# A hybrid attention/mLSTM layer on one core: the mLSTM output projection by a seven-product scheme

## The chip, the cores and the metric

The kernel runs on one core of a Trainium2 chip, as one launch. The metric is the device time of that launch in microseconds. Three runs of the kernel before took 1912.51 us in the median (1910.1 to 1913.47).

## The reference

One inference step of one layer, for a prompt of 512 tokens and 8 sample sequences of 8 tokens (T = 576 token columns together), model width 2048. Two mixers run side by side on one projection of the input, and are merged:

```
h = rmsnorm(x, norm_pre) * (1 + scale(c)) + shift(c)
u = h @ w_in                                   # columns: both mixers' inputs and the gates g_a, g_m
y_a = (att * silu(z_a)) @ w_br_a               # 1024 -> 2048, attention half of the branch
y_m = (sigmoid(o_m) * hm * silu(z_m)) @ w_br_m # 1024 -> 2048, mLSTM half of the branch
y = (sigmoid(g_a) * y_a + sigmoid(g_m) * y_m) @ w_out
out = x + gate(c) * rmsnorm(y, norm_post)
```

All is float32. Keys, values and the mLSTM state are outputs too, but the change does not touch them.

## The kernel before

A float32 product is computed as three products of rounded parts: each operand is split into a high part (`hi`, rounded by the scalar engine) and the rest (`lo`, subtracted by the vector engine), and TensorE adds hi*hi, hi*lo and lo*hi into PSUM. Work is written out by hand per engine, and the engines meet on counting semaphores. One step of the weight stream is called a granule, numbered x; `S_F` is the first granule of the branch, `S_G` the first of the last product `@ w_out`, `S_END` the end.

**The gate stage** (128 granules, just ahead of the branch) computes the two gates' columns with a seven-product scheme (Strassen's, in Winograd's form): a 2x2 block product in 7 instead of 8 block products. Its granule is 21 matmuls, 128x128 by 288 columns. SyncE loads raw weights for two granules at a time (two transfers of 256 KB, `form_load`, L584) into one of three buffers `w_all`. The vector engine builds four more weight forms by sums (`forms_a` L2201, `forms_b` L2206 and L2207), the scalar engine rounds (`f_hi`), the vector engine subtracts (`f_lo`, L2212). After 8 granules the seven PSUM results are combined on the vector engine (`products_a`, `products_b`, L2225 to L2244).

**The branch** (64 granules) is a plain product. The 2048 output features are taken in four quads of 512. Each quad has a half-matrix of 8 granules for attention (`ya`) and then one of 8 for mLSTM (`ym`), so that ya and ym alternate. A granule (`wide_granule`) is one row block of the weights, 128x512: 4 blocks of 3 matmuls with 512 prompt columns, and 2 for the 64 sample columns with the roles of the operands exchanged (`s_part`). At a half-matrix's end `mix` multiplies the four PSUM blocks by the gates (L2310) and adds ya and ym (L2315). The sample part is transposed back by 4 small matmuls (`fold_features`, L1190) one granule after the half-matrix's end. Raw weights come through a ring of four 256 KB slots, `w_raw`.

**The last product** (64 granules, also 14 matmuls each) takes its stationary operand from `y_all`, which is split from `g_a` in groups of four.

The order on the vector engine is that of one loop over x: in iteration x it makes the low part of granule x+3, then whatever else falls in that iteration. Each engine takes its instructions strictly in that order. The scalar engine's loop is the same with the high part, which waits until TensorE has used the slot.

Of the kernel before, what the change touches and what calls it, by code (L numbers as in the profile page):

```python
# [101 lines left out]
def mat_of(x):  # L102

    for m, (i, kind, first, n) in enumerate(MATS):
        if first <= x < first + n:
            return m, i, kind, x - first, n
# [24 lines left out]
def build(nc, x_prompt, x_sample, cache_k, cache_v, state_C, state_n, state_m, page_table, c_prompt, c_sample,  # L131
# [13 lines left out]
    with ctx:  # L145
# [36 lines left out]
        brm = [sb(f"brm{k}", "R3" if k < 4 else "R2", (4 + k if k < 4 else k - 4) * 2 * T, [P, 2 * T], F32R) for k in range(8)]  # L182
# [190 lines left out]
        g_a = wk("g_a", [P, 4, T], off=0)  # L373
        g_m = wk("g_m", [P, 4, T])
        s_copy = wk("s_copy", [P, QW], off=8 * T + QW)
# [14 lines left out]
        def back(q):  # L390
            if q < 4:
                return att_back[:, q % 2, :]
            return (y_back if q % 4 < 2 else rows_back)[:, q % 2, :]

        def wide_pair(x):
            if x >= S_END - 2:
                return end_hi[x - S_END + 2], end_lo[x - S_END + 2]
            return w_hi[:, slot_of(x)], w_lo[:, slot_of(x)]
# [70 lines left out]
        in_att, IN_ATT = (in_k, in_v), 32 * NB  # L469
        in_ga, IN_GA = in_n0, 16  # L470
# [14 lines left out]
        def _(sp):  # L485
# [80 lines left out]
            def load_rows(src, kt, col, slot):  # L566
                sp.dma_start(w_raw[:, slot].rearrange("p t c -> p (t c)"), src[kt * P:(kt + 1) * P, bass.ds(col, QW)])\
                  .then_inc(raw_ready[slot], 16)

# [20 lines left out]
            def branch_quad(i, n1):  # L590
                col_br = n1 * QW - QW
                for j in range(FGRAN):
                    sp.wait_ge(lo_ready, S_F + FGRAN * i + j - RING + 1)
                    if j < KT // 2:
                        load_rows(wba, j, col_br, slot_of(j))
                    else:
                        load_rows(wbm, j - KT // 2, col_br, slot_of(j))

            sp.wait_ge(lo_ready, S_F - 2)
            with sp.Fori(1, FQ + 1) as i:  # L600
                branch_quad(i - 1, i)

            def out_quad(q):
                col = sp.snap(q * QW)
                for kt in range(KT):
                    sp.wait_ge(lo_ready, S_G + q * KT + kt - RING + 1)
                    load_rows(wo, kt, col, slot_of(kt))

            with sp.Fori(0, FQ) as q:
                out_quad(q)  # L610
# [10 lines left out]
        def _(pe):  # L621
# [544 lines left out]
            def wide_granule(m, x, of, first, last):  # L1166

                hi, lo, both = of
                for b in range(4):
                    if first:  # L1170
                        if m:
                            pe.wait_ge(bank_free[b // 2], V0 + 32 + 2 * m - 1 + b % 2)
                        else:
                            pe.wait_ge(p_free, 7 * (GP - 1) + (4, 6, 7, 7)[b])
# [5 lines left out]
                if first and m:  # L1180
                    pe.wait_ge(s_copied, m)
# [11 lines left out]
            def branch_quad(i):  # L1193
                for j in range(FGRAN):
                    m, _, kind, kt, n = mat_of(S_F + FGRAN * i + j)
                    pe.wait_ge(lo_ready, S_F + FGRAN * i + j + 1)
                    if not i:
                        pe.wait_ge(br_lo, j + 1)
                    of = parts((bra if kind == "ya" else brm)[kt])
                    wide_granule(m, S_F + FGRAN * i + j, of, kt == 0, kt == n - 1)  # L1200
                    if kt == 1 and m:
                        fold_features(m - 1)

            for i in range(FQ):
                branch_quad(i)
# [11 lines left out]
            def out_quad(q, kts):  # L1217
                m = NM + q
                for kt in range(kts):
# [6 lines left out]
                    for tt in range(NT):  # L1226
                        if first:
                            pe.wait_ge(bank_free[tt // 2], V0 + 32 + 2 * m - 1 + tt % 2)
                        rows = slice(tt * P, (tt + 1) * P)
# [4 lines left out]
                    if first:  # L1234
                        pe.wait_ge(s_copied, m)
                    s_part(x, both, first, last)
                    if kt == 1 and not q:
                        fold_features(m - 1)
# [23 lines left out]
        def _(act):  # L1262
# [297 lines left out]
            def br_hi_of(q):  # L1560
# [8 lines left out]
                go((bra[q] if q < 8 else brm[q - 8])[:, 0:T], back(q)).then_inc(br_hi, 1)  # L1569

            def split_first(x):

                act.wait_ge(gemm_used, S_F - 2 if x < S_F + 2 else S_F)
                split_hi(slot_of(x), (x - GG) // RING, x)

            for g in range(GG):
# [14 lines left out]
                if g >= GG - 2:  # L1591
                    split_first(S_F + g - GG + 2)
# [819 lines left out]
        def _(pool):  # L2412
# [258 lines left out]
            for q in (2, 3, 4, 6):  # L2671
                back_load(q)
# [54 lines left out]
```

## Time and profile before

| | |
|---|---|
| median of 3 runs | 1912.51 us |
| profiled execution: its time / its span | 1909.96 us / 1908.5 us |
| TensorE busy | 1878.3 us (98%) |
| VectorE busy | 993.6 us (52%) |
| ScalarE busy | 684.5 us (36%) |
| gate stage | 1126 to 1484 us |
| branch | 1484 to 1692 us |
| last product | 1692 to 1901 us |

A busy engine is one that executes. Where a row of the timeline starts before the row above it has ended, the two overlap in the engine's pipeline: the distance from start to start is then what an instruction costs in a dense row, and its duration is when its result is there. Matmul ends are modelled.

### The profile page before, as it was taken

Reading aid. Unit: us, or ns where it says so; the run is one execution under the profiler, and the core shown is the slowest. Engines: PE = TensorE matmul, PEld = TensorE weight load, DVE = VectorE, ACT = ScalarE, POOL = GpSimd, SP = SyncE. Lnnn points to the kernel's source line nnn. Section 1 sums busy time; section 2 is a strip of 40 time slices with the busy share of each in tenths; the row PEclk is TensorE's granted clock in tenths of the full one; section 3 lists DMA queues with packets and bytes.
Section 4 is the critical chain, followed back from the end, with each engine's and each line's share of the span. In section 5 each row is a group of like instructions: output and inputs, shape, how many; then the busy total and the mean of one; then the engine's idle time right before and its main releaser. Section 6 shows DMA issues by size and latency. Waiting matters only on the chain.

```text
span 1908.5 us, 32997 instructions
## 1 busy us (share of the span) xinstructions
PE 1878.3 (98%) x13093; PEld 1684.8 (88%) x13093; DVE 993.6 (52%) x2026; ACT 684.5 (36%) x1136; POOL 201.9 (11%) x343
## 2 busy tenths in 40 slices
PE   6999999999999999999999999999999999999998
PEld 4779898988899999888899999999999888888886
DVE  4666234336563334554445767777777544443234
ACT  4312222234445453543333333344334422223332
POOL 2111001200002100111331000000000100000000
PEclk9999999999999999999999999999999999999999
DMA  9996573323224543233443334343444634443223
GB/s 318 319 288 200 186 228 112 78 67 101 55 83 141 172 155 100 74 84 120 118 138 94 104 119 124 113 125 118 133 121 125 230 128 133 132 166 95 83 78 132
DMA packets 188157, 261.88 MB, mean 137 GB/s; under 512 B 15706, under 2 KB 146906, under 8 KB 186858
## 3 DMA queue, kind: packets, MB, share of 16 engines
q1 hardware_dynamic: 167344, 194.03, 33.8%
q0 software_dynamic: 18432, 65.74, 10.4%
q8 instruction: 97, 1.59, 0.3%
q10 hardware_dynamic: 2242, 0.19, 0.1%
q14 instruction: 42, 0.34, 0.1%
HBM read 231.55 MB, written 28.35 MB: 136 GB/s over the span
## 4 chain that ended last, share of the span: by engine, by line
PE 93%; SPq 2%; DMA 2%; DVE 1%; POOL 1%; ACT 1%; issue 0%; DVEq 0%; ACTq 0%; POOLq 0%
PE gemm L623 67%; PE bank_s L623 12%; PE bank_a L623 6%; PE bank_o L623 5%; SPq L499 2%; DMA ada_in<-in_w_ada 1%; PE bank_s L876 1%; PE bank_s L652 1%; PE bank_a L820 0%; DVE y_tok L2397 0%; DMA w_raw<-in_w_in 0%; PE bank_s L1041 0%; POOL hm_sq L2595 0%; POOL hm_sq L2594 0%; PE bank_o L674 0%
## 5 line engine op out<-in xcount | busy, mean ns | idle before, releaser
L1264 ACT ACTIVATE w_hi<-w_raw 128x512 fp32r<-128x512 f32 x382 | 239.9, 629 | 689.3 <-PE gemm L623 406.7
L1676 DVE TENSOR_TENSOR w_lo<-w_raw,w_hi 128x512 fp32r<-128x512 f32 x382 | 268.4, 703 | 415.6 <-ACT w_hi L1264 415.0
L623 PE MATMUL gemm<-h_hi,w_hi 128*128 128x288 f32 x2048 | 461.1, 307 | 1.2 <-DVE dec_tok L1957 0.5
L623 PE MATMUL gemm<-h_hi,w_lo 128*128 128x288 f32 x2048 | 438.7, 296 | 0.0
L623 PE MATMUL gemm<-h_lo,w_hi 128*128 128x288 f32 x2048 | 437.3, 295 | 0.0
L623 PEld LDWEIGHTS gemm<-h_hi,w_hi 128*128 128x128 f32 x2048 | 328.2, 189 | 49.3 <-issue 42.8
L623 PEld LDWEIGHTS gemm<-h_hi,w_lo 128*128 128x128 f32 x2048 | 329.1, 188 | 0.0
L623 PEld LDWEIGHTS gemm<-h_lo,w_hi 128*128 128x128 f32 x2048 | 328.8, 188 | 0.0
L1264 ACT ACTIVATE f_hi<-w_all 128x896 fp32r<-128x896 f32 x128 | 120.0, 950 | 180.4 <-PE gemm L623 104.3
L2212 DVE TENSOR_TENSOR f_lo<-w_all,f_hi 128x896 fp32r<-128x896 f32 x128 | 139.4, 1089 | 63.5 <-ACT f_hi L1264 63.1
L623 PE MATMUL gemm<-w_hi,y_all 128*128 128x512 f32 x496 | 153.6, 391 | 0.0
L623 PEld LDWEIGHTS gemm<-w_hi,y_all 128*128 128x128 f32 x496 | 92.8, 188 | 22.9
L623 PE MATMUL gemm<-w_lo,y_all 128*128 128x512 f32 x248 | 96.7, 390 | 0.0
L623 PE MATMUL gemm<-bra,w_hi 128*128 128x512 f32 x256 | 79.4, 391 | 0.0
L623 PE MATMUL gemm<-brm,w_hi 128*128 128x512 f32 x256 | 79.4, 391 | 0.0
L623 PE MATMUL gemm<-s_hi,f_lo 128*128 128x288 f32 x256 | 75.6, 295 | 0.0
L623 PE MATMUL gemm<-s_hi,f_hi 128*128 128x288 f32 x256 | 75.4, 295 | 0.0
L623 PE MATMUL gemm<-s_lo,f_hi 128*128 128x288 f32 x240 | 70.8, 295 | 0.0
L1970 DVE CUSTOM_DVE_ANT_0 e_map<-bank_s,alibi 128x128 f32<-128x128 f32 (+3 forms) x64 | 31.4, 491 | 53.5 <-PE bank_s L623 52.3
L623 PEld LDWEIGHTS gemm<-bra,w_hi 128*128 128x128 f32 x256 | 47.7, 188 | 12.1 <-issue 0.2
L623 PEld LDWEIGHTS gemm<-brm,w_hi 128*128 128x128 f32 x256 | 47.7, 188 | 11.8 <-issue 0.2
L2643 POOL DMA_DIRECT2D gate_scratch<-h_free x32 | 22.1, 746 | 315.5 <-ACT h_free L1264 315.5
(538 smaller groups left out, 3112.5 us busy)
## 6 DMA issues: line engine op xcount, KB each, us to landing
w_raw<-in_w_in SPq DMA_DIRECT2D x256, 256.0 KB, 2.9
ada_in<-in_w_ada SPq DMA_DIRECT2D x72, 512.0 KB, 8.0
w_all<-in_w_in SPq DMA_DIRECT2D x128, 256.0 KB, 3.2
w_raw<-in_w_out SPq DMA_DIRECT2D x64, 256.0 KB, 2.5
gate_scratch<-h_free POOLq DMA_DIRECT2D x32, 288.0 KB, 3.1
ada_gate<-in_w_ada SPq DMA_DIRECT2D x16, 512.0 KB, 5.3
k_page<-in_cache_k POOLq DMA_DIRECT2D x16, 512.0 KB, 5.3
v_page<-in_cache_v POOLq DMA_DIRECT2D x16, 512.0 KB, 4.6
```

Of the source, the lines that this page charges most:

```text
L499: sp.dma_start(ada_slot(n)[:, :, half * CW:(half + 1) * CW], w_ada2[r * AQ * P:(r + 1) * AQ * P, col:col + CW] .rearrange("(t p) c -> p t ...
L623: return nc.tensor.matmul(out, lhsT, rhs, start=start, stop=stop, skip_group_check=True)
L652: nc.tensor.transpose(banks[0][:, j * P:(j + 1) * P], src[:, j * P:(j + 1) * P], ident[:])
L876: done = nc.tensor.transpose(bank_s[:, j // 2, (j % 2 * PAGES + pg) * P:(j % 2 * PAGES + pg + 1) * P], k_page[:, pg, h * P:(h + 1) * P], i ...
L1264: return nc.scalar.activation(out, in_, func, **kw)
L1676: V.tensor_tensor(w_lo[:, slot], w_raw[:, slot], w_hi[:, slot], ALU.subtract).then_inc(lo_ready, 1)
L1970: link(V.tensor_tensor_reduce(e_map[:, s % 2, c, 0:n], bank_s[:, c, 0:n], alibi[:, TP - n:TP], 1.0, LOW, ALU.add, ALU.max, mx[:, s % 2, c: ...
L2212: V.tensor_tensor(f_lo[wslot_of(g)][:], w_all[g // 2 % WRING][:, g % 2, P:8 * P], f_hi[wslot_of(g)][:], ALU.subtract).then_inc(lo_ready, 1)
L2643: pool.dma_start(gate_scratch[i // 8, 2 * (i % 8) + cb].rearrange("p (a t) -> p a t", a=2), h_free[:].rearrange("p (k e) t -> p k e t", e= ...
```

## The change

The mLSTM half of the branch is computed by the seven-product scheme, and the order of the half-matrices becomes ya0 to ya3, then ym0 to ym3. A ym granule (`pair_granule`) is 21 matmuls with 288 columns that cover prompt and samples alike; four such granules (the 1024 inputs are 8 row blocks, taken two by two) complete a pair of column blocks, 128 features each, and the seven results are combined (`m_products_a`, `m_products_b`) and gated (`gate_pair`, at the granules of a table, `GATED_AT`). The activations' sums and splits are made once, in the first two ya half-matrices (`brm_sums`, `brm_hi_of`, `brm_lo_of`). Raw ym weights for two granules at a time come into one of two buffers, `w_form`, of which the second lies over the whole of `w_raw`. `y_all` is split one block per granule, two granules ahead of its use, and the gates of ya lie in four buffers `y_f` that also hold the sum.

```diff
-MATS = [(i, kind, S_F + FGRAN * i + first, KT // 2) for i in range(FQ) for kind, first in (("ya", 0), ("ym", KT // 2))]
+BRANCH = (("ya", 0), ("ya", 1), ("ya", 2), ("ya", 3), ("ym", 0), ("ym", 1), ("ym", 2), ("ym", 3))
+MATS = [(i, kind, S_F + FGRAN * k, FGRAN) for k, (kind, i) in enumerate(BRANCH)]
+KX = KT // 4
+GATED_AT = ((0, MATS[4][2] + 5), (1, MATS[5][2] + 1), (2, MATS[5][2] + 5), (3, MATS[6][2] + 1), (4, MATS[6][2] + 5),
+            (5, MATS[7][2] + 1), (6, S_G + 1), (7, S_G + 3))
...
+        w_form = [sb("w_form0", "h_hi", 0, [P, 2, 8 * P]), sb("w_form1", "w_raw", 0, [P, 2, 8 * P])]
...
 # SyncE
+            def pair_load(k, b):
+                i, _, first, _ = MATS[k]
+                x = first + 2 * b
+                if b % 2:
+                    sp.wait_ge(lo_ready, RAW_FREE[x])
+                elif k == 4 and not b:
...
+                else:
+                    sp.wait_ge(lo_ready, x - 2 if b else form_before(k) + 6)
+                col = i * QW + b // 2 * CW
+                for s in range(2):
+                    row = (4 * (b % 2) + 2 * s) * P
+                    sp.dma_start(w_form[b % 2][:, s, 0:4 * P].rearrange("p (t c) -> p t c", t=2),
+                                 wbm[row:row + 2 * P, col:col + CW].rearrange("(t p) c -> p t c", p=P)).then_inc(in_form[b % 2], 16)
...
 # TensorE
+            def pair_granule(m, a, n, j, x):
+                pe.wait_ge(lo_ready, x + 1)
+                if not n:
+                    pe.wait_ge(br_lo, KT // 2 + j + 1)
+                wh, wl = f_hi[SLOT[x]], f_lo[SLOT[x]]
+                for k, (of, part) in enumerate(((0, 0), (5, 4), (2, 1), (4, 5), (6, 2), (3, 3), (1, 6))):
+                    if j == 0:
+                        bank_wait(m, a, n, k)
+                    cols = slice(of * P, (of + 1) * P)
+                    hi, lo = brm_hi[j][:, part, :], brm_lo[j][:, part, :]
+                    for i, (w, h) in enumerate(((wh, hi), (wh, lo), (wl, hi))):
+                        done = mm(m_banks[k], w[:, cols], h, start=j == 0 and i == 0, stop=j == KX - 1 and i == 2)
+                    if j == KX - 1 and k < 6:
+                        done.then_inc(p_done, 1)
+                done.then_inc(gemm_used, 1)
...
 # ScalarE
+            def pair_hi(x):
+                b = mat_of(x)[3] // 2
+                act.wait_ge(m_made, ...)
+                act.wait_ge(gemm_used, SLOT_FREE[x])
...
+                go(f_hi[SLOT[x]][:], w_form[b % 2][:, x % 2, P:8 * P]).then_inc(hi_ready, 1)
...
 # VectorE
+            def gate_pair(n):
...
+                link(V.scalar_tensor_tensor(c, g, 1.0, c, ALU.add, ALU.mult))
+                V.tensor_tensor(y, y, c, ALU.add).then_inc(mix_ready, 1)
...
             for x in range(S_F, S_END):
                 m, i, kind, kt, n = mat_of(x)
-                if x + LOOKAHEAD < S_END - 2:
-                    split_lo(slot_of(x + LOOKAHEAD), x + LOOKAHEAD)
...
+                ends = kind == "ym" and kt % KX == KX - 1
+                y = x + LOOKAHEAD
+                sums = is_form(y) and mat_of(y)[3] % 2 == 0
...
+                if sums:
+                    pair_a(b)
+                    if not ends:
+                        pair_b(b)
+                if ends:
+                    m_products_a(2 * i + kt // KX)
+                if is_form(x + 2):
+                    pair_lo(x + 2)
+                if ends:
+                    m_products_b(2 * i + kt // KX, x)
+                    if sums:
+                        pair_b(b)
...
+                if y < S_END - 2 and not is_form(y) and not (late and kt == n - 2):
+                    row_lo(y)
...
+                if x - S_F - 6 in range(0, 2 * KX, 2):
+                    brm_sums((x - S_F - 6) // 2)
+                if x - S_F - 7 in range(0, 2 * KX, 2):
+                    brm_lo_of((x - S_F - 7) // 2)
...
+                for n_pair, at in GATED_AT:
+                    if x == at:
+                        gate_pair(n_pair)
...
+                if kind == "ya" and kt == n - 1:
+                    mix(a)
```

Two places on the vector engine show how it lands in the program. First, the middle of the branch. Before, from the end of a ya half-matrix (`g_a`) to that of the ym half-matrix after it (`g_m`):

```order
L2310 SCALAR_TENSOR_TENSOR g_a<-g_a,gemm 128x512 x4
L1676 TENSOR_TENSOR w_lo<-w_raw,w_hi 128x512 x3
L2320 TENSOR_REDUCE s_copy<-bank_s 128x256
L2328 SCALAR_TENSOR_TENSOR g_a<-g_a,s_copy 128x4x64
L1676 TENSOR_TENSOR w_lo<-w_raw,w_hi 128x512 x5
L2310 SCALAR_TENSOR_TENSOR g_m<-g_m,gemm 128x512 x4
L2315 TENSOR_TENSOR g_a<-g_a,g_m 128x512 x4
```

Eight granules need eight `w_lo`, and the gating stands once per half-matrix.

Now, in the ym half-matrices, four granules make one cycle. This is its first half, the iteration that forms the weights of the next two granules but one, with a gating in it (`w_form_77` and `w_form_78` are the two buffers, `c_buf` the combined results):

```order
L2491 TENSOR_TENSOR w_form_77<-w_form_77 128x2x256
L2496 TENSOR_TENSOR w_form_77<-w_form_77 128x2x128
L2497 TENSOR_TENSOR w_form_77<-w_form_77 128x2x128
L2503 TENSOR_TENSOR f_lo_110<-w_form_78,f_hi_107 128x896
L2550 SCALAR_TENSOR_TENSOR c_buf_258<-g_m,c_buf_258 128x1152
L2551 TENSOR_TENSOR y_f_73<-y_f_73,c_buf_258 128x1152
L2503 TENSOR_TENSOR f_lo_109<-w_form_77,f_hi_106 128x896
```

The fourth row is the last reader of buffer 78, so that its next load starts behind it; the second half of the cycle begins with the forms in that buffer:

```order
L2491 TENSOR_TENSOR w_form_78<-w_form_78 128x2x256
L2517 TENSOR_TENSOR m_u_80<-m_p_79,bank_o 128x288
L2521 TENSOR_TENSOR c_buf_259<-m_p_79,gemm 128x288
L2524 TENSOR_TENSOR m_u_81<-m_u_80,gemm 128x288
L2503 TENSOR_TENSOR f_lo_111<-w_form_77,f_hi_108 128x896
L2531 TENSOR_TENSOR c_buf_259<-m_u_81,gemm 128x288
L2533 TENSOR_TENSOR c_buf_259<-m_u_81,gemm 128x288
L2534 TENSOR_TENSOR m_u_80<-m_u_80,gemm 128x288
L2537 TENSOR_TENSOR c_buf_259<-m_u_80,bank_s 128x288
L2496 TENSOR_TENSOR w_form_78<-w_form_78 128x2x128
L2497 TENSOR_TENSOR w_form_78<-w_form_78 128x2x128
L2503 TENSOR_TENSOR f_lo_110<-w_form_78,f_hi_107 128x896
```

The last two rows of sums stand directly ahead of the low part that is made from them.

Second, the end of the first ya half-matrix, iteration S_F+7. Before (`brm` are mLSTM activations, split as they come):

```order
L1676 TENSOR_TENSOR w_lo<-w_raw,w_hi 128x512
L2172 TENSOR_TENSOR brm_67<-rows_back,brm_67 128x512
L2173 TENSOR_TENSOR brm_67<-rows_back,brm_67 128x64
L2310 SCALAR_TENSOR_TENSOR g_a<-g_a,gemm 128x512 x4
L1676 TENSOR_TENSOR w_lo<-w_raw,w_hi 128x512
```

And now:

```order
L2442 TENSOR_TENSOR w_lo<-w_raw,w_hi 128x512
L2482 TENSOR_TENSOR brm_lo_69<-y_back,brm_hi_65 128x288
L2483 TENSOR_TENSOR brm_lo_69<-y_back,brm_hi_65 128x576
L2485 TENSOR_TENSOR brm_lo_69<-m_new,brm_hi_65 128x1152
L2565 SCALAR_TENSOR_TENSOR y_f_73<-y_f_73,gemm 128x512 x4
L2442 TENSOR_TENSOR w_lo<-w_raw,w_hi 128x512
```

Larger splits of activations stand ahead of the four operations that free the PSUM blocks.

## Rows read from the trace of the kernel before

**Rows 1.** The page, busy time and share of each engine:

```profile
PE 1878.3 (98%) x13093; PEld 1684.8 (88%) x13093; DVE 993.6 (52%) x2026; ACT 684.5 (36%) x1136; POOL 201.9 (11%) x343
```

**Rows 2.** Windows: length, busy (count) by engine, PE clock, DMA share, GB/s:

```profile
1236.00:1484.00 248.00, 248.00 (x1872) 247.96 (x1870) 188.45 (x306) 100.59 (x116) 17.71 (x26) 1.00 0.41 122
1484.00:1692.00 208.00, 207.96 (x927) 167.69 (x926) 98.27 (x179) 59.21 (x97) 10.26 (x14) 1.00 0.44 148
```

**Rows 3.** The chain that ended last: start us, us, what:

```profile
1137.66 1.20 PE gemm L623 x9
...
1296.40 1.20 PE gemm L623 x9
...
1506.86 2.73 PE gemm L623 x12
...
1510.06 2.72 PE gemm L623 x12
...
1516.42 0.44 PE bank_s L1190 x4
1516.86 2.75 PE gemm L623 x12
...
1542.86 2.75 PE gemm L623 x12
```

**Rows 4.** Timeline, VectorE, gate stage: start, us, operation [idle before <- releaser]:

```profile
1415.51 0.45 DVE L2225 TENSOR_TENSOR h_free<-h_free,bank_s 128x288 f32<-128x288 f32 x1 [0.95 <-ACT h_free L1264]
...
1416.61 1.08 DVE L2212 TENSOR_TENSOR f_lo<-w_all,f_hi 128x896 fp32r<-128x896 f32 x1
1417.61 0.45 DVE L2238 TENSOR_TENSOR h_free<-h_free,gemm 128x288 f32<-128x288 f32 x1
...
1418.89 0.46 DVE L2244 TENSOR_TENSOR h_free<-h_free,gemm 128x288 f32<-128x288 f32 x1
1419.26 0.42 DVE L2206 TENSOR_TENSOR w_all<-w_all 128x256 f32<-128x256 f32 x1
...
1421.16 1.09 DVE L2212 TENSOR_TENSOR f_lo<-w_all,f_hi 128x896 fp32r<-128x896 f32 x1 [1.02 <-ACT f_hi L1264]
1422.17 0.68 DVE L2201 TENSOR_TENSOR w_all<-w_all 128x512 f32<-128x512 f32 x1
1422.89 0.43 DVE L2206 TENSOR_TENSOR w_all<-w_all 128x256 f32<-128x256 f32 x1
...
1423.69 1.08 DVE L2212 TENSOR_TENSOR f_lo<-w_all,f_hi 128x896 fp32r<-128x896 f32 x1
```

**Rows 5.** Timeline, ScalarE, the same stretch:

```profile
1420.17 0.95 ACT L1264 ACTIVATE f_hi<-w_all 128x896 fp32r<-128x896 f32 x1 [3.92 <-DVE w_all L2207]
...
1421.87 1.15 ACT L1264 ACTIVATE h_free<-h_free 128x1152 f32<-128x1152 f32 x1
```

**Rows 6.** Groups of instructions by form, VectorE: count | busy us, mean ns | idle:

```profile
L2192 DVE TENSOR_TENSOR s_lo<-s_new,s_hi 128x1152 fp32r<-128x1152 f32 x7 | 9.5, 1352 | 0.0
```

**Rows 7.** Loads of `w_all`: one pair's issues; landing of all, 1239.9's, 1269.3's:

```profile
L584 SPq DMA_DIRECT2D w_all<-in_w_in x2: 368/424/479, 1424.8 to 1425.2; - x2
DMA to landing us min/median/max: 2.7/3.2/5.4
DMA to landing us min/median/max: 3.2/3.2/3.2
DMA to landing us min/median/max: 3.7/3.7/3.7
```

**Rows 8.** Timeline at S_F+7, ScalarE and VectorE:

```profile
1506.96 0.63 ACT L1264 ACTIVATE w_hi<-w_raw 128x512 fp32r<-128x512 f32 x1 [1.99 <-PE bank_s L623]
1507.50 0.67 ACT L1264 ACTIVATE brm<-rows_back 128x576 fp32r<-128x576 f32 x1
...
1508.97 2.47 DVE L2310 SCALAR_TENSOR_TENSOR g_a<-g_a,gemm 128x512 f32<-128x512 f32 x4
```

**Rows 9.** Windows, the start of the program; columns as in rows 2:

```profile
10.00:20.00 10.00, 5.72 (x30) 5.72 (x31) 4.78 (x10) 7.46 (x9) 1.21 (x3) 1.00 1.09 301
```

More of the change, by code:

```diff
@@ L588, in _ @@
                 form_load(b)
[L590 to L601, printed above, removed]
@@ new lines, in form_before @@
+            def form_before(k):
+                return max(first for _, kind, first, _ in MATS[:k] if kind == "ym")
+            for k, (i, kind, first, n) in enumerate(MATS[:len(BRANCH)]):
+                then = MATS[k + 1][1]
+                if kind == "ya":
+                    for j in range(n):
+                        if j or not follows_form(first):
+                            row_load(wba, first + j, j, i * QW)
+                        if j == 3 and then == "ym":
+                            pair_load(k + 1, 0)
+                    if then == "ym":
+                        pair_load(k + 1, 1)
+                else:
+                    for b in range(0 if MATS[k - 1][1] == "ym" else 2, 4):
+                        if b == 3 and then != "ym":
+                            row_load(wba if then == "ya" else wo, first + n, 0, MATS[k + 1][0] * QW)
+                        pair_load(k, b)
@@ L605, in out_quad @@
+            for q in range(FQ):
                 for kt in range(KT):
[L606 to L610, printed above, removed]
+                    if q or kt:
+                        row_load(wo, S_G + q * KT + kt, kt, q * QW)
             for nth, tt in enumerate(LAST_ORDER):
@@ L1164, in s_part, with pairs_before, wide_granule @@
                 mm(bank_s[0:NS, 0, :], both[:, 0:NS], wl, start=False, stop=last).then_inc(gemm_used, 1)
-            def wide_granule(m, x, of, first, last):
+            def pairs_before(m):
+                return GP + sum(2 for _, kind, _, _ in MATS[:m] if kind == "ym")
+            def wide_granule(m, a, x, of, first, last):
                 hi, lo, both = of
@@ L1191, in fold_features @@
                 done.then_inc(s_folded, 1)
[L1193 to L1202, printed above, removed]
@@ new lines, in _ @@
+            a = n = 0
+            for m, (i, kind, first, count) in enumerate(MATS[:len(BRANCH)]):
+                for kt in range(count):
+                    if kind == "ya":
+                        pe.wait_ge(lo_ready, first + kt + 1)
+                        if not m:
+                            pe.wait_ge(br_lo, kt + 1)
+                        wide_granule(m, a, first + kt, parts(bra[kt]), kt == 0, kt == count - 1)
+                    else:
+                        pair_granule(m, a, n + kt // KX, kt % KX, first + kt)
+                    if kt == 1 and m and MATS[m - 1][1] == "ya":
+                        fold_features(a - 1)
+                if kind == "ya":
+                    a += 1
+                else:
+                    n += 2
@@ new lines, in _ @@
+                if ends:
+                    m_products_b(2 * i + kt // KX, x)
+                    if sums:
+                        pair_b(b)
+                b += sums
+                if y < S_END - 2 and not is_form(y) and not (late and kt == n - 2):
+                    row_lo(y)
+                elif S_END - 2 <= y < S_END:
+                    end_split_lo(y)
+                if 4 <= x - S_F + 3 < 8:
+                    br_lo_of(x - S_F + 3)
+                if x - S_F - 6 in range(0, 2 * KX, 2):
+                    brm_sums((x - S_F - 6) // 2)
```

408 lines of the change are left out of this document (283 added, 125 removed).

## The prediction

> **What bounds the kernel now.** I read the page's busy times first: TensorE is busy 98% of the span, VectorE 52% [rows 1]. Then the windows by stage: in the gate stage TensorE is busy 248.0 of 248 us with VectorE at 188 (76%), in the branch 207.96 of 208 with VectorE at 98 (47%) [rows 2]. So TensorE sets both paces, but the stage that already uses the seven-product scheme has much less room beside it. Third, the chain of waits for the price of a granule [rows 3]. In the gate stage the same piece starts at 1137.66 and, 57 granules later, at 1296.40: 2.785 us for 21 matmuls of 288 columns. In the branch two granules start 3.195 us apart, for 14 matmuls of 512 columns, a half-matrix takes 1542.86 - 1516.86 = 26.00 us, and of that 0.44 us is the four transposes of the sample part. Last, the timelines of VectorE and ScalarE in the gate stage, because the change puts that pattern where results are combined twice as often.
>
> **TensorE alone.** 32 ym granules go from 3.195 to 2.785 us: -13.1 us. The transposes stand after 8 half-matrices before and after 4 now: -1.8 us. Together -14.9 us, if TensorE never waits.
>
> **What VectorE has to do.** Costs are distances from start to start in dense stretches of rows 4. Per granule one `f_lo` of 896 columns: 1421.16 to 1422.17, 1.01 us. Per two granules the forms: `pair_a` 0.72 (1422.17 to 1422.89), `pair_b` 0.80 (1422.89 to 1423.69). Per four granules the seven combinations: three take 1415.51 to 1416.61, 1.10 us, four 1417.61 to 1419.26, 1.65 us. The gate stage pays those once in eight granules. New is `gate_pair`, two dependent operations of 1152 columns: one such takes 1.352 us [rows 6]; the first counts with 0.04 more for the wait between them, the second with 0.08 less for the overlap, 2.66 us. Six of the eight fall inside the ym stretch.
>
> Now the cycle of four granules in the order in which the change's rows stand. Half one: forms 1.52, `f_lo` 1.01, `gate_pair` 2.66, `f_lo` 1.01: 6.20 us. Half two: `pair_a` 0.72, then what the gate stage shows word for word: 1415.51 to 1422.17, 6.66 us, for the three combinations, an `f_lo`, the four combinations, `pair_b`, and an `f_lo`. That stretch holds an idle 1.02 us [rows 4]: `pair_b` comes last, the next `f_lo` needs the high part of just these forms, and ScalarE starts it only at `pair_b`'s end, 0.95 us of work [rows 5]. Half two is 7.38 us. The cycle is 13.6 us, and TensorE needs 4 x 2.785 = 11.1 us. In the gate stage this hole is hidden by eight granules' room (22.3 us); here it is not.
>
> **The load inside the cycle.** The gate stage has three weight buffers, the ym stage two. A buffer's load starts when the `f_lo` of its second granule ends; VectorE has in between only one `f_lo`, and the gating in half one, before it stands at the forms that need the data. From that end to the issue 0.03 us, the second transfer is issued 0.4 later (1424.8, 1425.2), and it lands after 3.2 us in the pair at 1239.9, 3.7 in that at 1269.3, 3.4 in the mean of nine pairs [rows 7]: 3.88 us in all, with the wake-up. Half one then takes 1.52 + 1.09 + 3.88 = 6.49 us instead of 6.20. In half two the load (0.72 + 1.10 + 1.09 + 3.88 = 6.79) fits in 7.38. Cycle: 13.9 us. Bounds: with the fastest landing of 2.7 the load is hidden and the cycle is 13.6; at 5.4 it lasts through both halves, 8.5 + 8.8 = 17.3 us. I take the mean of the nine, since the ym stretch has fewer other transfers than the gate stage with its stores.
>
> [...]
>
> **The ym stretch, summed.** Zero is TensorE's start of the first ym granule. VectorE has the first two granules ready by then; the third's high part must wait until TensorE has left the last ya granule, so the first regular forms start at 0.95 + 0.08 + 1.01 = 2.0 us. The first cycle has no gating but the samples' reduction of ya3, about 1.1 us, and waits once for ScalarE: I follow it through to 14.6 us. Five more cycles, 69.5, to 86.1. The last forms' cycle frees TensorE's last bank only by its fourth combination: 6.49 + 0.72 + 1.10 + 1.00 + 1.28 + 0.46 = 11.1, then one product 0.4 and three granules 8.4, in all 19.9. TensorE leaves ym at 106.0 us. By itself it would need 32 x 2.785 + 0.44 = 89.6, so +16.4 us. The first two granules of the last product wait 0.8 us for the last combinations and low parts.
>
> **The end of the first ya half-matrix.** In iteration S_F+7 the splits of the first mLSTM activations stand ahead of `mix` on VectorE. Before, `mix` began at 1508.97, 2.0 us after ScalarE's `w_hi` of that granule (1506.96), and 1.1 us before TensorE wanted the first block, at 1510.06 [rows 3, 8]. Now ScalarE first rounds 288, 576 and 1152 columns: it starts on them 0.54 after `w_hi` [rows 8] and needs about 0.30 + 0.57 + 1.15 (1.15 for 1152 columns [rows 5]; the others are durations of 0.41 and 0.67 less the overlap). VectorE follows with 0.37 + 0.67 + 1.27 (1.352 less 0.08), and the first block of `mix` takes 0.68. From TensorE's start of the granule: 0.10 + 0.54 + 2.02 + 0.04 + 2.31 + 0.68 = 5.7 us, where TensorE comes for the block at 3.2. It waits 2.5 us, once; the later ends of ya have no such splits. At the least it is 0, if ScalarE's roundings ran ahead (its loop does not let them), at the most about 4 with a late load of the rows.
>
> **What costs nothing.** The splits of `y_all` (0.74 on VectorE, 0.6 on ScalarE per granule) stand in granules where VectorE has 0.6 of 3.2 us to do; the two gatings in the last product add 2.7 each and use up the lead there, not more. The cover is two granules of lead; without it they would cost about 1 us each. POOL and SyncE only issue.
>
> **Sum.** -14.9 + 16.4 + 0.8 + 2.5 = +4.8 us. The profiled execution took 1909.96, so it would take 1914.8; against the median 1912.51 that is 1917.3 us. The profiled execution lies 2.6 us under the median, inside the spread of the three.
>
> **The rivals.** (1) VectorE keeps up and TensorE sets the pace: -14.9 + 2.5, 1900 us. For it: the gate stage runs this pattern with TensorE never idle. Against: 13.6 us of VectorE's queue per 11.1 us. It would need the gating to cost nearly nothing and the hole of 1.02 to close. 10%. (2) The load is hidden and `mix` is not late: -14.9 + 14.6 + 0.8, 1913 us: 22%. For it: landings of 2.7 to 3.0 occur. (3) The side of a clear loss: the loads land late. One place: the forms of half one behind the pair's landing. Three gate loads of 1152 KB run while pairs are on their way, and landings of 5.4 have been seen [rows 7]. From a landing of 3.2 on each 0.1 us costs 0.6 us, from 4.0 on both halves wait and it is twice that. At 4.1 it gives +10, 1922 us; 17%. (4) TensorE's clock falls to the lower level, 1.2 GHz, in the holes. At half the clock the ym matmuls need about 178 us instead of 106, so 1990 us. Against: in 10 to 20 us of the program TensorE was busy 5.72 of 10 us with the granted clock at 1.00 [rows 9], and my holes are a fifth of the time. 3%. The Trainium skill (TensorE: Matmul & The Clock Gate, "Part 1") says that idle time sends the clock to half rate; rows 9 show none of it at a lower busy share. (5) The change does less than it says: the order of the program shows the 21 matmuls, so nothing here. Other mishaps 3%.
>
> **How the numbers follow.** The forecast, VectorE's queue with the load in it and a late first `mix`, has 45%, its own range 1914 to 1920. A change within 0.2% (3.8 us) can't be told from none. Slower by more: most of the forecast's case (0.38), (3), (4) and mishaps, 0.60. Within: the rest of it and (2), 0.30. Faster: (1), 0.10. The range 1910 to 1926 leaves out (1), (4) and the far end of (3).
>
> **What would show it.** Right: in the ym stretch `f_lo` of half two idle about 1 us on ScalarE; VectorE over 85% busy there; TensorE about 84%, idle for `f_lo` and the combinations; cycles of 13.9 us; forms waiting a few tenths for the load every second time; one wait of 2.5 us for the first `mix`. The forecast is wrong if TensorE is above 95% busy between the first ym granule and the last product, or if that stretch is under 100 or over 111 us.

## The result and the profile after

The changed kernel takes 1916.17 us in the median of 15 runs (1913.39 to 1918.77), the kernel before 1910.91 in 15 runs beside it (1909.2 to 1913.47): ratio 1.0027, 95% interval 1.002 to 1.0034. It is 5.3 us slower by the medians, where the forecast was +4.8 us and 1917.3. The profiled execution of the changed kernel took 1913.39 us (span 1911.9), the fastest of its 15, and 3.4 more than that of before. In that pair the three parts of the program can be compared: up to TensorE's first matmul of the branch -0.8 us (1484.24 and 1483.40), the branch +4.3 (207.6 and 211.9), the last product the same (216.6 both).

The page's busy times, which answer to [rows 1]:

```profile
PE 1870.1 (98%) x13301; PEld 1689.6 (88%) x13301; DVE 1055.7 (55%) x2114; ACT 697.6 (36%) x1144; POOL 201.2 (11%) x343
```

TensorE has 8 us less to do and the kernel is slower, so the time is in waits. The windows by stage (columns as in [rows 2]) say where. The first is ya, the second ym, the third the last product:

```profile
1484.00:1590.00 106.00, 103.33 (x460) 83.09 (x459) 57.95 (x98) 33.60 (x52) 7.98 (x11) 1.00 0.50 173
1590.00:1697.00 107.00, 98.58 (x684) 91.58 (x683) 91.51 (x147) 34.20 (x46) 2.25 (x3) 1.00 0.34 113
1697.00:1904.00 207.00, 206.80 (x921) 166.21 (x920) 84.87 (x141) 66.97 (x129) 5.30 (x9) 1.00 0.33 110
```

In ym TensorE is busy 98.6 of 107 us, 92% (matmul ends are modelled; by its dense distances it has 89.6 us to do in a stretch of 105.3, 85%, and the waits below are the surer sign), VectorE 91.5 of 107 (86%); in the branch of before VectorE had 98 of 208 [rows 2]. Ya has one hole of 2.7 us. One full ym cycle on VectorE (start us, us, operation, and in brackets the idle time ahead of it and who ended it), from the forms of one pair of column blocks to those of the next:

```profile
1606.58 0.69 DVE L2491 TENSOR_TENSOR w_form<-w_form 128x512 f32<-128x512 f32 x1
...
1608.11 1.08 DVE L2503 TENSOR_TENSOR f_lo<-w_form,f_hi 128x896 fp32r<-128x896 f32 x1
1609.11 1.35 DVE L2550 SCALAR_TENSOR_TENSOR c_buf<-g_m,c_buf 128x1152 f32<-128x1152 f32 x1
1610.49 1.36 DVE L2551 TENSOR_TENSOR y_f<-y_f,c_buf 128x1152 f32<-128x1152 f32 x1
1611.77 1.08 DVE L2503 TENSOR_TENSOR f_lo<-w_form,f_hi 128x896 fp32r<-128x896 f32 x1
1612.77 0.68 DVE L2491 TENSOR_TENSOR w_form<-w_form 128x512 f32<-128x512 f32 x1
1613.49 0.45 DVE L2517 TENSOR_TENSOR m_u<-m_p,bank_o 128x288 f32<-128x288 f32 x1
...
1617.70 0.42 DVE L2497 TENSOR_TENSOR w_form<-w_form 128x256 f32<-128x256 f32 x1
1619.14 1.09 DVE L2503 TENSOR_TENSOR f_lo<-w_form,f_hi 128x896 fp32r<-128x896 f32 x1 [1.02 <-ACT f_hi L1394]
1620.15 0.68 DVE L2491 TENSOR_TENSOR w_form<-w_form 128x512 f32<-128x512 f32 x1
```

1620.15 - 1606.58 = 13.57 us: 12.55 of dense work and one idle 1.02, the same hole, at the same place, as in [rows 4]. What TensorE waits for in ym, by the waits of 1590 to 1697 (us in total, times, longest; PE is its matmuls, PEld its weight loads), and what the forms wait for; then the landings of the 26 transfers into `w_form` that SyncE issues from 1595 on, each from its own issue:

```profile
PEld gemm L707 <- DVE c_buf L2531: 5.2, 6, 0.9
PEld bank_o L707 <- DVE m_u L2517: 4.0, 6, 0.7
PE gemm L707 <- DVE c_buf L2531: 3.9, 6, 0.7
PE bank_o L707 <- DVE m_u L2517: 2.6, 6, 0.4
PE bank_a L707 <- DVE f_lo L2503: 0.8, 2, 0.6
DVE w_form L2491 <- DMA w_form<-in_w_br_m: 0.9, 1, 0.9
```

```profile
DMA to landing us min/median/max: 2.7/3.0/4.9
```

The combinations stand too late in VectorE's queue six times, the load is late once. The waits of the matmuls sum to 7.3 us, those of the weight loads to 14.0 (with 3.0 for `f_lo` and 1.8 for `m_u` of L2534), and the stretch is 15.7 us longer than 89.6. At iteration S_F+7, rows of ScalarE, VectorE and TensorE, which answer to [rows 8]:

```profile
1506.68 1.00 ACT L1394 ACTIVATE brm_hi<-y_back 128x288 fp32r<-128x288 f32 x2
1507.59 1.15 ACT L1394 ACTIVATE brm_hi<-m_new 128x1152 fp32r<-128x1152 f32 x1
...
1509.81 1.35 DVE L2485 TENSOR_TENSOR brm_lo<-m_new,brm_hi 128x1152 fp32r<-128x1152 f32 x1
1511.08 2.48 DVE L2565 SCALAR_TENSOR_TENSOR y_f<-y_f,gemm 128x512 f32<-128x512 f32 x4
...
1511.91 0.70 PE L707 MATMUL gemm<-bra,w_hi 128*128 128x512 f32 x2 [2.67 <-DVE y_f L2565]
```

`mix` starts 2.1 us later than before, and TensorE waits 2.67 us.

### The profile page after: what moved, and what is told of

The parts are those of the page before. It is cut to its first block, busy times and chain, and to the rows that moved or that the text cites. A ratio compares the mean times of both kernels' runs of the same rounds, so it can differ in the third digit from the quotient of the medians.

```text
span 1911.9 us, 33182 instructions
## 1 busy us (share of the span) xinstructions
PE 1870.1 (98%) x13301; PEld 1689.6 (88%) x13301; DVE 1055.7 (55%) x2114; ACT 697.6 (36%) x1144; POOL 201.2 (11%) x343
## 3 DMA queue, kind: packets, MB, share of 16 engines
q0 software_dynamic: 18432, 65.74, 10.2%
## 4 chain that ended last, share of the span: by engine, by line
PE 88%; DVE 5%; DMA 2%; ACT 1%; issue 1%; POOL 1%; SPq 1%; DVEq 0%; ACTq 0%; POOLq 0%
PE gemm L707 62%; PE bank_s L707 11%; PE bank_a L707 6%; PE bank_o L707 5%; DVE f_lo L2503 1%; PE bank_s L960 1%; SPq L556 1%; DMA ada_in<-in_w_ada 1%; PE bank_s L736 1%; PE bank_a L904 0%; DVE y_tok L2670 0%; DVE y_f L2551 0%; DMA w_raw<-in_w_in 0%; DVE w_form L2491 0%; DVE c_buf L2550 0%
## 5 line engine op out<-in xcount | busy, mean ns | idle before, releaser
L1394 ACT ACTIVATE w_hi<-w_raw 128x512 fp32r<-128x512 f32 x349 | 219.1, 629 | 615.4 <-PE gemm L707 406.5
L1840 DVE TENSOR_TENSOR w_lo<-w_raw,w_hi 128x512 fp32r<-128x512 f32 x256 | 181.3, 709 | 177.2 <-ACT w_hi L1394 176.6
L2442 DVE TENSOR_TENSOR w_lo<-w_raw,w_hi 128x512 fp32r<-128x512 f32 x93 | 64.3, 692 | 158.6 <-ACT w_hi L1394 158.5
L707 PEld LDWEIGHTS gemm<-w_lo,y_all 128*128 128x128 f32 x248 | 46.6, 188 | 9.9
```

Of the source, the lines that this page charges most:

```text
L707: return nc.tensor.matmul(out, lhsT, rhs, start=start, stop=stop, skip_group_check=True)
L1394: return nc.scalar.activation(out, in_, func, **kw)
L1840: V.tensor_tensor(w_lo[:, slot], w_raw[:, slot], w_hi[:, slot], ALU.subtract).then_inc(lo_ready, 1)
L2442: V.tensor_tensor(w_lo[:, SLOT[x]], raw_of(x), w_hi[:, SLOT[x]], ALU.subtract).then_inc(lo_ready, 1)
```

## The experiments

Twelve kernels were run, each with five timed rounds beside the kernel before. The kernel before took 1909.5 to 1910.9 us in the medians of these sets, so kernels are compared by their ratios, not by their times. e2, e4 and e9 leave out most of the gating of six pairs. "Stretch" is the time from TensorE's first ym matmul to its first matmul of the last product in the profiled execution; in the changed kernel it is 1695.3 - 1590.0 = 105.3 us. The theory was the forecast's: in ym the cycle is VectorE's queue with the load inside it. Its rivals: the queue alone, the load alone, TensorE's own count.

| kernel | us | ratio to before [95%] | stretch |
|---|---|---|---|
| changed | 1916.17 | 1.0027 [1.002, 1.0034] | 105.3 |
| e1 `mix` first | 1911.68 | 1.0013 [1.0004, 1.0022] | 105.3 |
| e2 no gating | 1915.37 | 1.0036 [1.0023, 1.005] | 105.5 |
| e3 three buffers | 1914.66 | 1.0024 [1.0013, 1.0036] | 104.6 |
| e4 both | 1902.67 | 0.9966 [0.9952, 0.9979] | 93.2 |
| e5 sums early | 1915.77 | 1.0029 [1.0018, 1.0041] | 105.5 |
| e6 `f_lo` first | 1915.44 | 1.0028 [1.0016, 1.0039] | 106.3 |
| e7 three edits | 1912.39 | 1.0013 [1.0004, 1.0022] | 106.3 |
| e8 gating spread | 1905.67 | 0.9979 [0.997, 0.9988] | 100.0 |
| e9 e4 and `mix` first | 1899.78 | 0.9945 [0.9932, 0.9959] | 92.6 |
| e10 gating deferred | 1904.15 | 0.9968 [0.9957, 0.9979] | 94.4 |
| e11 one place earlier | 1905.41 | 0.9975 [0.9966, 0.9984] | 94.7 |
| e12 none just ahead | 1900.83 | 0.9953 [0.994, 0.9967] | 94.8 |

**e1, `mix` ahead of the low parts of its iteration**

```diff
+                if kind == "ya" and kt == n - 1:
+                    mix(a)
+                    a += 1
                 if x - S_F - 7 in range(0, 2 * KX, 2):
                     brm_lo_of((x - S_F - 7) // 2)
...
-                if kind == "ya" and kt == n - 1:
-                    mix(a)
-                    a += 1
```

> The changed kernel with the four operations of `mix` of the first ya half-matrix ahead of the mLSTM activations' low parts on VectorE. If the 2.7 us that TensorE waits there are on the path, the time falls by 2.7 us (ratio to before from 1.0027 to 1.0013) and TensorE's wait for y_f is gone. The rival, that VectorE only gets the same work later and the wait comes back before the ym stretch or in it, expects no change (1.0027).

TensorE's wait on `y_f` is gone from the trace, and the ratio is the expected one: 0.0014 or 2.7 us under the changed kernel, with intervals that allow some 0.5 to 5 us. From TensorE's first matmul of the branch to its first of ym it is 103.7 us (1483.99 to 1587.66) instead of 106.6 (1483.40 to 1589.99), 2.9 less. What is late in ya is that order.

**e2, e3, e4: the gating away, a third buffer, both**

```diff
 # e2: gating operations of six pairs on one column
+                if n < 6:
+                    c, g, y = c[:, 0:1], g[:, 0:1], y[:, 0:1]
                 link(V.scalar_tensor_tensor(c, g, 1.0, c, ALU.add, ALU.mult))
 # e3: three buffers, taken in turn
-        w_form = [sb("w_form0", "h_hi", 0, [P, 2, 8 * P]), sb("w_form1", "w_raw", 0, [P, 2, 8 * P])]
+        w_form = [sb("w_form0", "h_hi", 0, [P, 2, 8 * P]), sb("w_form1", "w_raw", 0, [P, 2, 8 * P]), sb("w_form2", "R1", 0, [P, 2, 8 * P])]
+        OF = [g % 3 for g in range(15)] + [1]
```

> Leaves out the gating of the six pairs that is done inside the ym stretch, but for one column of each (part of y is missing). Theory of the queue alone: each cycle of four granules on VectorE shrinks from 13.6 by 2.4 us to 11.2, TensorE nearly sets the pace, 6 x 2.4 = 14 us less (ratio 0.995). Theory of queue and load: with the gating gone the forms of every first half stand waiting for the load (1.5 + 1.1 + 3.5 = 6.1 us instead of 6.2), the cycle stays at 13.4 to 13.5 and the time falls by about 1 us (ratio 1.002).

> A third buffer for the raw ym weights, the gating as in the changed kernel. Both theories expect little: the loads are hidden already but for one wait of 0.9 us, so 0 to 1 us less (ratio 1.0022 to 1.0027). If the loads set the pace in a way that the waits don't show, it would fall by more than 3 us.

> Leaves out the same gating and has the third buffer. Both theories now expect VectorE's cycle at 11.2 us and the ym stretch near TensorE's own 89.6 us: 14 us less than the changed kernel, ratio 0.995. If the queue alone was right, it equals the run without gating; if queue and load, it is 13 us below it. If neither, TensorE still waits and the stretch stays over 95 us.

In e2 2.4 of the 2.66 us of gating are gone from each cycle, and nothing is won; 1.0036 is even above the 1.002 that the theory gave, and its interval leaves that value out; the stretch is the same (105.5 and 105.3), so what is slower lies elsewhere, and it stays open. The timeline of VectorE in e2 shows who takes the gating's place:

```profile
1608.89 0.69 DVE L2491 TENSOR_TENSOR w_form<-w_form 128x512 f32<-128x512 f32 x1
...
1611.68 1.09 DVE L2503 TENSOR_TENSOR f_lo<-w_form,f_hi 128x896 fp32r<-128x896 f32 x1
1614.94 0.69 DVE L2491 TENSOR_TENSOR w_form<-w_form 128x512 f32<-128x512 f32 x1 [2.18 <-DMA w_form<-in_w_br_m]
...
1621.32 1.09 DVE L2503 TENSOR_TENSOR f_lo<-w_form,f_hi 128x896 fp32r<-128x896 f32 x1 [1.02 <-ACT f_hi L1394]
1622.32 0.69 DVE L2491 TENSOR_TENSOR w_form<-w_form 128x512 f32<-128x512 f32 x1
```

The cycle is 13.43 instead of 13.57: the forms stand 2.18 us at the load that the gating had covered (14.8 us over the stretch). The gain is all in half one, 6.05 us from forms to forms instead of 6.19; half two is 7.38 in both. The third buffer alone (e3) takes away the one wait of 0.85 us and leaves the cycle at 13.57. Both together take 12 us out of the stretch. In e4, from forms to forms:

```profile
1607.84 0.69 DVE L2496 TENSOR_TENSOR w_form<-w_form 128x512 f32<-128x512 f32 x1
...
1618.00 1.09 DVE L2508 TENSOR_TENSOR f_lo<-w_form,f_hi 128x896 fp32r<-128x896 f32 x1 [1.02 <-ACT f_hi L1399]
1619.01 0.69 DVE L2496 TENSOR_TENSOR w_form<-w_form 128x512 f32<-128x512 f32 x1
```

11.17 us. That is VectorE's own queue without the gating (13.57 - 2.40), the hole of 1.02 included, and it is TensorE's own 4 x 2.785 = 11.14 from [rows 3] too. TensorE waits for VectorE only 2.1 us in all, at the last load, so here the hole costs nothing that shows. e4 was expected at 0.995 and is 0.9966 [0.9952, 0.9979]; its stretch is 3.6 us over 89.6, with a wait of 3.1 us on VectorE for that last load.

So in half one the queue (6.19) and the load (6.05) bound the cycle side by side, and either alone may go without effect; in half two the queue with its hole bounds alone. In the changed kernel itself it is the queue that binds; the load stands 0.14 us behind it. Of the rivals, the load alone falls by e3, the queue alone by e2, and TensorE's own count by e4.

**e5 and e6: filling the hole**

```diff
 # e5
                     pair_a(b)
-                    if not ends:
-                        pair_b(b)
+                    pair_b(b)
 # e6
+                if is_form(x + 2):
+                    pair_lo(x + 2)
                 if sums:
                     pair_a(b)
+                    pair_b(b)
```

> Both combinations of a pair stand before the forms in every iteration, so that VectorE has work while ScalarE makes f_hi; the 1.02 us hole of each mLSTM cycle is filled. If the VectorE queue alone set the cycle of 13.57 us, six cycles lose 1.1 us each: ratio 0.999. If queue plus load set it (the next load goes out when f_lo is done, and takes 3.0 us), the second half has then only 1.52 + 1.10 + 1.09 us of work for a way of 6.5 to 7.2 us from f_lo to the next forms, and nearly all that is won comes back as a wait on the load: -0.2 us a cycle, ratio 1.002. If TensorE's own count set it, nothing: 1.003.

> f_lo of the next pair first in the iteration, then the combinations, then the forms. By queue plus load the load starts earlier and more of the second half's work lies beside it: cycle 12.5 us in place of 13.57, -1.1 x 6 to 7 = -7 us: ratio 0.999. If the order of the queue does not matter because VectorE's sum of work alone sets the cycle (11.4 to 12.5 us busy), the hole only moves elsewhere: 1.0027.

e5 came out as queue plus load wants (1.0029 for 1.002, inside its interval): the 1.02 is gone, and the forms of the other half now wait for their load, 7.1 us in seven waits (e5, VectorE):

```profile
1610.77 0.69 DVE L2491 TENSOR_TENSOR w_form<-w_form 128x512 f32<-128x512 f32 x1 [0.85 <-DMA w_form<-in_w_br_m]
```

Cycle 1603.57 to 1616.96, 13.39 us. e6 is a miss: I expected 0.999 and it is 1.0028. With `f_lo` first the loads are early enough, and no form waits for one. But the combinations now stand behind an `f_lo` and the forms, TensorE waits for their first, gives its operand slot back later, and ScalarE's next high part is late for that. The wait over e6's stretch, then ScalarE and VectorE:

```profile
PE bank_o L707 <- DVE m_u L2517: 11.1, 7, 1.6
```

```profile
1607.02 0.95 ACT L1394 ACTIVATE f_hi<-w_form 128x896 fp32r<-128x896 f32 x1 [2.76 <-PE bank_s L707]
```

```profile
1608.00 1.09 DVE L2503 TENSOR_TENSOR f_lo<-w_form,f_hi 128x896 fp32r<-128x896 f32 x1 [0.79 <-ACT f_hi L1394]
```

The hole has moved and is 0.79 us long; the cycle is 1601.67 to 1615.19, 13.52 us. Load, operand slot and PSUM banks each tie the order of the queue, and in each of the three orders so far one of them leaves VectorE idle. Its own work is 12.55 us in the changed kernel, 12.73 in e6 and 12.75 in e8 below, of a cycle that TensorE wants in 11.1.

**e7 and e8: the three edits, and the gating spread**

e7 is e1 and e6 together, with the last pair's combinations ahead of the rows of S_G+1, on ScalarE too. In e8, built on e7, `f_lo` stands first, then the combinations, then the forms; `GATED_AT` has two places for each gating, one per operation, each pair has its own `c_buf`, and the gates `g_m` have two buffers that are loaded earlier:

```diff
 # e7
+                if late and kt == n - 1:
+                    row_lo(x + 2)
 # e8
+GATED_AT = ((0, MATS[4][2] + 7, MATS[5][2] + 1), (1, MATS[5][2] + 7, MATS[6][2] + 1), (2, MATS[6][2] + 7, MATS[7][2] + 1),
+            (3, MATS[7][2] + 3, MATS[7][2] + 5), (4, S_G + 1, S_G + 1), (5, S_G + 3, S_G + 3), (6, S_G + 5, S_G + 5), (7, S_G + 7, S_G + 7))
+        c_buf = [sb(f"c_buf{n}", "R1" if n < 4 else "R3", n % 4 * 2 * T, [P, 2, T]) for n in range(NP)]
+                if first:
+                    link(V.scalar_tensor_tensor(c, g, 1.0, c, ALU.add, ALU.mult))
+                if last:
+                    V.tensor_tensor(y, y, c, ALU.add).then_inc(mix_ready, 1)
```

> e6, and mix ahead of brm_lo of its stage (-2.7 us by the wait on y_f), and the combinations of the last pair ahead of the rows of S_G+1, which stand on a load that starts 5 us before the end of the stretch (-1 us). The three are on different stretches and should add: -10 to -11 us against the changed kernel, ratio 0.997. If the slack of one is used up by another, e.g. the output stage waits elsewhere, 0.999.

> e7, with the gating of the branch outputs (5.6 us a cycle at two ops a half) taken apart: a buffer of its own for each pair, the gating of four pairs moved out of the mLSTM stretch into the output stage, where VectorE has idle time, and the rest one half later. If VectorE's queue with its loads is all that keeps the stretch above TensorE's count, the cycle falls to 11.4 to 12.0 us (e4 without the gating: 11.37), the stretch to 93 to 96 us and the ratio to 0.992 to 0.994, below the kernel before. If the output stage has no room for the 11 us of VectorE work, it comes back there: 0.998.

e7 is a miss (expected 0.997). It has e1's ratio to the fourth digit: its other two edits together do nothing that can be measured. e8 beats the kernel before, but it is a miss as well: 0.9979 instead of 0.992 to 0.994, its stretch 100.0 instead of 93 to 96 us. The output stage gave nothing back: from its first matmul to the end it takes 216.5 us, as in the changed kernel (216.6). The cycles are longer than the 11.4 to 12.0 that I gave. Its two kinds of cycle, VectorE:

```profile
1602.29 0.68 DVE L2491 TENSOR_TENSOR w_form<-w_form 128x512 f32<-128x512 f32 x1
...
1604.91 2.09 DVE L2503 TENSOR_TENSOR f_lo<-w_form,f_hi 128x896 fp32r<-128x896 f32 x2 [1.02 <-ACT f_hi L1394]
...
1609.55 1.09 DVE L2503 TENSOR_TENSOR f_lo<-w_form,f_hi 128x896 fp32r<-128x896 f32 x1 [1.02 <-ACT f_hi L1394]
...
1614.77 0.69 DVE L2491 TENSOR_TENSOR w_form<-w_form 128x512 f32<-128x512 f32 x1
...
1627.52 0.68 DVE L2491 TENSOR_TENSOR w_form<-w_form 128x512 f32<-128x512 f32 x1
```

With a gating the cycle is 1614.77 to 1627.52, 12.75 us, without any idle time on VectorE: that is the floor of the queue with all of the cycle's work in it, and 0.8 us under the changed kernel's cycle. Without a gating it is 12.48, since that order leaves the hole open twice. e8 moves gatings and changes the order in one, so its gain of 0.0034 over e7 is not divided between the two.

**e9: the cover taken away altogether**

> e4 (third w_form buffer, and the gating operations of six pairs cut to one column, so the gating is left out there) with mix ahead of brm_lo and the last pair's combinations ahead of the rows of S_G+1. It asks what the change would give if VectorE kept up: -14.9 us by TensorE's own count. Theory: all that stood against it is the queue with its loads and the late mix, so -2.7 for mix, -1 for the last pair and some of the 1.5 us wait after the last two-buffer load (stays): 1902.7 - 4 = 1899, ratio 0.994 to 0.995. If the TensorE count itself is mis-sized, the wait on y_f only moves and the ratio stays at 0.9966.

1899.78 us, 0.9945. This is the case of the forecast's first rival (VectorE keeps up), brought about, with `mix` in time besides. TensorE's count gives -14.9 us for it and it is 10.2 under the kernel before in its set (1910.01); its stretch of 92.6 us is still 3.0 over 89.6. Its gating of six pairs is left out, so it is no candidate.

**e10, e11, e12: all the work, in another place**

e10 has e9's order and third buffer, six buffers `c_buf` and e8's two buffers `g_m`; the three differ in where the gatings stand (e11 and e12 are shown against e10; e11's other places are e10's):

```diff
 # e10
+GATED_AT = ((0, MATS[4][2] + 7, MATS[5][2] + 1), (1, MATS[5][2] + 7, MATS[6][2] + 1), (2, S_G - 1, S_G - 1), (3, S_G, S_G),
+            (4, S_G + 2, S_G + 2), (5, S_G + 4, S_G + 4), (6, S_G + 6, S_G + 6), (7, S_G + 7, S_G + 7))
 # e11
-            (2, S_G - 1, S_G - 1), (3, S_G, S_G)
+            (2, MATS[7][2] + 5, MATS[7][2] + 5), (3, S_G - 1, S_G - 1)
 # e12
+            (2, MATS[7][2] + 5, MATS[7][2] + 5), (3, S_G + 1, S_G + 1),
+            (4, S_G + 3, S_G + 3), (5, S_G + 5, S_G + 5), (6, S_G + 6, S_G + 6), (7, S_G + 7, S_G + 7)
```

> All of the work is done. Third w_form buffer, mix ahead of brm_lo, the last pair's combinations ahead of the rows, and of the eight gatings only those of pairs 0 and 1 stay in the mLSTM stretch; the other six stand in the first eight granules of the output stage and in the iteration ahead of it. The cycles without gating should take TensorE's 11.37 us, as in e4; with it about 1.4 more, twice: stretch 95 to 97 us (e8: 100.0). Output stage: 6 x 2.65 = 16 us of gating in 8 granules x 3.55 = 28 us, where VectorE has about 10 us to do: it fits by the sum, and the two gatings that stand in neighbouring iterations may cost up to 2 us. Ratio 0.995 to 0.996, under e8's 0.9979. If the output stage gives the time back, 0.998.

> e10 with two gatings one place earlier: that of pair 2 in the last mLSTM half-matrix, that of pair 3 in the iteration ahead of the output stage. In e10's trace the two neighbouring gatings and the last combinations hold y_all of the second output block back: TensorE waits 2.72 us there, and in the 4 us after it the granted clock is 0.58, which makes the next matmuls 1.05 in place of 0.62 us per two. Theory: with the queue 2.66 us shorter there, the wait goes and the clock stays at 1.00, -2.7 -1.4 us, and +1.4 us for a third cycle with gating: 1904.15 - 2.7 = 1901.5, ratio 0.9955. If the low clock comes from the change of stage and not from the wait, it is still there without it: 1903, ratio 0.9962.

> e11 left the wait where it was (3.36 us), because a gating still stands in iteration S_G-1, ahead of y_all's second block. Here none stands in S_G-1 or S_G: pair 2 in the last mLSTM half-matrix, pairs 3 to 7 at S_G+1, +3, +5, +6, +7. Theory: the second block's split then starts right behind the last combinations, 2.66 us earlier, TensorE waits under 0.7 us for it, and the granted clock stays at 1.00 behind it: the step from the last product's first granule to its third is 6.5 us in place of 9 (e10) and 10 (e11): 1904.15 - 2.7 - 1.4 + 1.4 = 1901.5 us, ratio 0.9955. If what is taken away there only comes back at S_G+5 to +7, where three gatings stand one behind the other: 0.997.

e10's stretch is 94.4 us, as wanted, but its ratio is 0.9968 instead of 0.995 to 0.996: its last product takes 220.8 us, 4.0 more than e9's 216.8. TensorE at its second block, and the windows behind it (columns as above; the PE clock is the third number from the end):

```profile
1687.98 0.70 PE L712 MATMUL gemm<-w_hi,y_all 128*128 128x512 f32 x2 [2.72 <-DVE y_all L2562]
1688.85 1.05 PE L712 MATMUL gemm<-w_hi,y_all 128*128 128x512 f32 x2
```

```profile
1684.00:1688.00 4.00, 1.28 (x7) 0.71 (x5) 3.97 (x6) 1.69 (x3) 0.00 (x0) 1.00 0.40 133
1688.00:1692.00 4.00, 4.00 (x11) 3.13 (x12) 3.97 (x6) 0.00 (x0) 0.59 (x1) 0.58 0.19 66
```

e11 is a miss that I could have read in the order: the split of the second block stands in iteration S_G-1 too, behind the gating that I had put there. TensorE waited 3.36 us, the clock fell again (0.81 and 0.76 in the two windows of 1688 to 1696), and the last product took 221.5 us. e12 has no gating in S_G-1 or S_G:

```profile
1686.31 0.70 PE L712 MATMUL gemm<-w_hi,y_all 128*128 128x512 f32 x2 [0.69 <-DVE y_all L2562]
```

```profile
1684.00:1688.00 4.00, 3.31 (x16) 2.36 (x15) 4.00 (x9) 1.56 (x3) 0.00 (x0) 1.00 0.44 138
1688.00:1692.00 4.00, 4.00 (x19) 3.27 (x18) 3.96 (x6) 1.21 (x2) 0.75 (x1) 1.00 0.41 126
```

1900.83 us, ratio 0.9953 where 0.9955 was expected. Its last product takes 217.2 us. The kernel does all of the work and beats the kernel before by 9 us, with 2.2 us of stretch more than e9.

## Why the prediction was right

- **TensorE's price, 2.785 us a granule.** Right: in e4, where hardly anything holds it, TensorE starts a granule every 2.76 to 2.83 us in most of the stretch.
- **The cycle, 13.9 us with the load in it.** The queue part was right to 0.03 (13.57 against 13.6), the load too dear: I took 3.4 us for the landing, from nine pairs, where the median of all transfers in [rows 7] is 3.2; in ym it was 3.0, and the forms waited for a load once (0.85 us), not in every cycle. That the load lengthens half one was the wrong part of the mechanism; it stays 0.14 us under the queue (e2). Five cycles took 1675.43 - 1606.58 = 68.9 us, forecast 69.5.
- **The first and the last cycle.** The first forms stood at 2.7 us instead of 2.0, and their cycle took 13.9 instead of 14.6, with the one wait for ScalarE (1.54 us, at 1596.81): 16.6 by both. From the last forms to the end of ym it took 1695.34 - 1675.43 = 19.9, as forecast. In all the stretch was 105.3 us against 106.0.
- **The last product's start.** 1698.89 - 1695.34 = 3.55 and 1702.17 - 1698.89 = 3.28, against 3.195: 0.4 us, forecast 0.8. Not foreseen: the last combinations stand behind the low part of a row whose load can start only at 1690.1, after the last `f_lo`. e7 moves them ahead, and its last product takes 216.5 us against 216.6: nothing that can be measured.
- **The late first `mix`, 2.5 us.** 2.67 in the trace. The price of the wait is larger in most profiles, because of the clock: from TensorE's first matmul of the branch to its first of ym it is 103.7 us in e1 without the wait, 106.6 in the changed kernel and e6, where the clock stayed at 1.00, and 108.0 to 108.2 in e2, e3, e4 and e5, where it fell. So the wait costs 2.9 us or 4.3 to 4.5.
- **The clock**, whose fall through the whole stretch I had given 3%, did not fall in the 1 us holes of ym: 1.00 in that window. Where it did fall is the 2.7 us wait in ya, for some 4 us at a time. That mechanism was in no term of the sum.
- **The signs.** VectorE's 86%, the idle 1.02 us, the one long wait for `mix` and a stretch inside 100 to 111 us came as said. TensorE's busy share came as 92% by the windows, not 84% (85% by distances), and the waits of the forms every second time did not come.
- **Rival (2)** (load hidden and `mix` not late, 1913) had its first half nearly right: over five cycles the load cost 0.9 us (68.9 against 5 x 13.6), where I had 1.5. Its second half was wrong.

With the terms as the profiled execution has them the sum is -14.9 + 15.7 + 0.4 + 2.7 = +3.9 us, and branch and last product together took 4.2 more than before. So the load (0.6) and the last product's start (0.4) were put too dear. The medians differ by 5.3. What lies between fits the clock after the wait, 1.4 to 1.6 us in the executions where it falls, but that is inferred: only profiled executions have windows. That the forecast of +4.8 is within half a microsecond of the medians is therefore in part luck, from errors of opposite sign. The step that was mis-sized is the late `mix`: its term has the wait, and not what the clock does after it.

## What to carry to other kernels

A stretch can be bound by an engine's queue and by a load inside that queue at once. Taking away either then shows nothing (e2, e3, e5), and neither result proves that it is harmless; take both away in one run before you drop the idea. Count the dense work of the second engine over one cycle of the first: where it is the larger, the order within the cycle can win the idle time at most (13.57 to 12.75 here, and e5 to e7 did not win even that), and work has to leave the stretch (e8, e12). And when work is moved, look what stands behind it in the very iteration that it lands in (e11).

## What the runs showed of the hardware

One wait, two outcomes. The same wait of 2.67 us ahead of the first `mix` stands in the traces of the changed kernel, e2, e3, e4, e5 and e6. Windows of 4 us behind it show a granted clock of 1.00 in the changed kernel and in e6, 0.57 in e2, e3 and e4, and 0.60 in e5: TensorE's lower level of 1.2 GHz after a single wait, and 1.00 again in the window after that. The window of e4, and of the changed kernel:

```profile
1512.00:1516.00 4.00, 4.00 (x13) 3.10 (x12) 3.46 (x8) 0.00 (x0) 0.00 (x0) 0.57 0.66 211
```

```profile
1512.00:1516.00 4.00, 4.00 (x18) 3.24 (x19) 3.82 (x8) 0.55 (x2) 0.17 (x1) 1.00 0.62 195
```

In e4 the granule after the wait lasts from 1511.56 to 1516.43, 4.87 us in place of 3.195: the wait of 2.67 us costs 4.3. The mean granted clock of every run is known too, though not where in the run it fell: it is 0.999 in four of the changed kernel's 15 runs, which took 1913.4 to 1914.3 us, and 0.996 to 0.998 in the others, which took 1913.6 to 1918.8. That fits; but the kernel before, without that wait, spreads over 4 us as well, at 0.997 to 0.999, and the clock falls elsewhere too: in e5 to 0.57 at 68 to 72 us of the program, in e7 to 0.78 and 0.79 at 64 to 72. So which single run had the low clock behind `mix` is not shown. The waits of 2.72 us in e10 and 3.36 in e11 were followed by it too; behind those of up to 1.6 us in e6's ym the granted clock is 1.00. What decides it at 2.67 us stays open.

The second: a hand-over from VectorE to ScalarE and back (forms, 0.95 us of `f_hi`, `f_lo`) with nothing between leaves VectorE idle for 1.02 us, alike in the gate stage of before [rows 4] and in the ym stretch of the changed kernel, e2, e4 and e8.
